# First projection of a hybrid transformer layer in two halves of its contraction, with tokens loaded first

## The reference, cut to what matters

```python
mod = silu(c) @ w_ada + b_ada
shift1, scale1, gate1, shift2, scale2, gate2 = split(mod, 6)
h = rmsnorm(x, norm1_g) * (1.0 + scale1) + shift1
proj = h @ w_in                       # q, v, forget gates, output gate, u (conv), branch gates
```

## Time and profile before

| | us |
|---|---|
| median of 3 runs | 834.47 |
| range of them | 833.5 to 837.01 |
| profiled execution, its own time | 835.81 |
| its span, first to last instruction | 834.0 |

### The profile page before, as it was taken

One profiled execution on the slowest core, in us unless ns is written; L12 is line 12 of the kernel. 1 busy time (PEld: TensorE's weight loads), 2 busy tenths in 40 slices (PEclk: granted clock), 3 DMA queues, 4 the chain that ended last, 5 costly groups with the idle time before them and its releaser, 6 DMA issues.

```text
span 834.0 us, 12875 instructions
## 1 busy us (share of the span) xinstructions
PE 793.0 (95%) x5234; PEld 545.1 (65%) x5234; DVE 381.6 (46%) x773; ACT 236.2 (28%) x400; POOL 20.9 (3%) x22
## 2 busy tenths in 40 slices
PE   4999999999999999999999999799999999989984
PEld 2779897999999999965555455354554745445222
DVE  1176999879987755583232312212222112112114
ACT  3163747344445353231111111111111101011001
POOL 1000010100000100100000000000000000000000
PEclk9999999999999999999999999999999999999998
DMA  8998797523442479869999999999999999999995
GB/s 331 408 362 332 283 410 293 194 101 103 152 152 101 152 236 372 369 233 423 391 425 426 421 426 426 422 425 426 421 427 420 422 423 425 423 425 425 426 420 202
DMA packets 81221, 284.71 MB, mean 341 GB/s; under 512 B 5256, under 2 KB 12040, under 8 KB 64520
## 3 DMA queue, kind: packets, MB, share of 16 engines
q1 hardware_dynamic: 80664, 282.55, 85.2%
q10 hardware_dynamic: 496, 1.30, 0.4%
HBM read 280.67 MB, written 3.16 MB: 340 GB/s over the span
## 4 chain that ended last, share of the span: by engine, by line
PE 64%; SPq 18%; DMA 11%; DVE 2%; issue 2%; ACT 1%; POOL 0%; DVEq 0%; POOLq 0%
SPq L628 14%; PE bank L2112 13%; PE bank L2168 7%; PE bank L1727 6%; PE bank L1729 6%; PE bank L1732 6%; DMA chunk<-in_w_expert_down 5%; PE bank L2019 3%; PE bank L1996 3%; PE bank L1789 3%; PE bank L1713 3%; PE bank L1771 3%; DMA chunk<-in_w_expert_gate_up 2%; PE bank L1674 2%; DMA ring<-in_w_out 2%
## 5 line engine op out<-in xcount | busy, mean ns | idle before, releaser
L2112 PE MATMUL bank<-chunk,xg 128*64 128x512 f32 (+2 forms) x1024 | 196.9, 602 | 8.9 <-DMA chunk<-in_w_expert_gate_up 8.7
L2112 PEld LDWEIGHTS bank<-chunk,xg 128*64 128x64 f32 (+2 forms) x1024 | 62.2, 127 | 136.9 <-issue 121.9
L2168 PE MATMUL bank<-chunk,act_t 128*64 128x512 f32 (+2 forms) x480 | 98.2, 620 | 3.7 <-DMA chunk<-in_w_expert_down 3.6
L1526 DVE SCALAR_TENSOR_TENSOR act_r<-bank,w_slot,sil 128x256 f32<-128x256 f32 x26 | 12.6, 484 | 166.1 <-ACT sil L995 166.1
L1538 DVE TENSOR_TENSOR y_lo<-bank,y_hi 128x512 fp32r<-128x512 f32 x52 | 35.8, 691 | 76.5 <-ACT y_hi L1008 76.5
L995 ACT ACTIVATE sil<-bank 128x256 f32<-128x256 f32 x26 | 10.0, 384 | 194.7 <-PE bank L2112 194.7
L1090 DVE TENSOR_TENSOR ring_lo<-ring,ring_hi 128x1024 fp32r<-128x1024 f32 x44 | 52.9, 1219 | 23.5 <-ACT ring_hi L777 23.3
L2168 PEld LDWEIGHTS bank<-chunk,act_t 128*64 128x64 f32 (+2 forms) x480 | 30.0, 131 | 51.2 <-issue 50.3
L1008 ACT ACTIVATE y_hi<-bank 128x512 fp32r<-128x512 f32 x52 | 30.9, 597 | 104.8 <-PE bank L2168 100.4
L1150 DVE SCALAR_TENSOR_TENSOR conv<-upad,dw,conv 128x256 f32<-128x256 f32 x120 | 52.8, 512 | 0.0
L777 ACT ACTIVATE ring_hi<-ring 128x1024 fp32r<-128x1024 f32 x44 | 44.4, 1054 | 27.3 <-PE bank L1753 12.6
(11 more groups left out here) (316 smaller groups left out, 1205.6 us busy)
## 6 DMA issues: line engine op xcount, KB each, us to landing
chunk<-in_w_expert_gate_up SPq DMA_DIRECT2D x128, 1024.0 KB, 20.2
chunk<-in_w_expert_down SPq DMA_DIRECT2D x63, 1024.0 KB, 22.3
ring<-in_w_in SPq DMA_DIRECT2D x16, 2048.0 KB, 9.7
ring<-in_w_ada SPq DMA_DIRECT2D x12, 2048.0 KB, 9.8
ring<-in_w_proj_hgrn SPq DMA_DIRECT2D x2, 2048.0 KB, 7.6
ring<-in_w_out SPq DMA_DIRECT2D x2, 2048.0 KB, 14.1
ring<-in_w_proj_conv SPq DMA_DIRECT2D x1, 2048.0 KB, 7.7
chunk<-in_w_shared_gate_up SPq DMA_DIRECT2D x2, 1024.0 KB, 22.8
```

Of the source, the lines that this page charges most:

```text
L2112: ins = mm(bank[2 + b][row:row + width, :], xg[:, k, c:c + width], w[:, k % 4, :], start=(k == 0), stop=(k == KD - 1))
L2168: ins = mm(out[row:row + width, :], act_t[:, c, row:row + width], w[:, c, h * 512:(h + 1) * 512], start=(c == 0), stop=(c == 1))
```

## The change

The contraction of `u1` is done in two halves. The first (k 0 to 3) needs only the scale of ada2, the second (k 4 to 7) that of ada3. So ada2 and ada3 get groups, partial banks, copies, sums and modulations of their own. The tokens are loaded ahead of ada2, and u1 ahead of ada3. On ScalarE the sigmoid goes behind the squares; on VectorE the scaling of the sum goes ahead of the silu; on TensorE the partial of ada2 goes behind h0 and h1. The counts of semaphores move with it. The diff, cut to its core:

```diff
-        ADA_GROUPS = ((0, 2), (2, 2), (4, 8))
+        ADA_GROUPS = ((0, 1), (1, 1), (2, 2), (4, 8))
...
-        for name in ("ada2", "ada3", "u1", "ada0", "ada1", "u2", ...
+        for name in ("ada2", "u1", "ada3", "ada0", "ada1", "u2", ...
+        place["u1"], place["ada3"] = 2, 1
@@ SP
-            load_block("ada2")
             for s, x in enumerate((A["x_prompt"], A["x_sample"])):
                 sp.dma_start(x_tok[:, s, :], x[0]).then_inc(s_x, 16)
+            load_block("ada2")
@@ ScalarE
-            act.wait_ge(vec_copied, 1)
-            nc.scalar.activation(csig, vec[:, R_C:R_C + 16], ACT.Sigmoid).then_inc(c_sig, 1)
...
             act.wait_ge(s_x, 32)
             for s in range(NS):
                 own.mark(nc.scalar.activation(xn[:, s, :], x_tok[:, s, :], ACT.Square, accum_out=ssq[:, s:s + 1]))
+            act.wait_ge(vec_copied, 1)
+            nc.scalar.activation(csig, vec[:, R_C:R_C + 16], ACT.Sigmoid).then_inc(c_sig, 1)
...
             copy_partials(0)
             act.wait_ge(s_init, 3)
-            act.wait_ge(gain1_done, 2)
             for j in (1, 3):
+                act.wait_ge(gain1_done, j + 1)
                 filled(act, f"h{j}")
...
                 ins.then_inc(act_evac, 1)
+                if j == 1:
+                    copy_partials(1)
...
             evacuate_u1(0)
-            copy_partials(1)
-            act.wait_ge(mod_done, 4)
+            copy_partials(2)
+            act.wait_ge(mod_done, 6)
@@ VectorE
+            dve.wait_ge(own_act, 2)
+            V.tensor_scalar(ssq, ssq, 1.0 / D, EPS, ALU.mult, ALU.add).then_inc(ssq_ready, 1)
             dve.wait_ge(vec_copied, 2)
             dve.wait_ge(c_sig, 1)
...
-            dve.wait_ge(own_act, 2)
-            V.tensor_scalar(ssq, ssq, 1.0 / D, EPS, ALU.mult, ALU.add).then_inc(ssq_ready, 1)
             dve.wait_ge(rms_ready, 1)
...
-            modulation(8, 16, 1, 2)
-            (gain1 of k 0 to 7, both kinds of token)
             for j in (0, 2):
+                modulation(8 + 2 * j, 12 + 2 * j, 1 + j // 2, 2 + j)
+                (gain1 of k 2j to 2j + 3, both kinds of token)
+                dve.wait_ge(gain1_done, 2 + j)
                 filled(dve, f"h{j}")
@@ TensorE
-            pe.wait_ge(vec_copied, 2)
-            pe.wait_ge(c_silu, 1)
-            ada_partial(0)
             pe.wait_ge(s_x, 32)
             for j in range(4):
                 to_channels((f"xt{j}", 0), x_tok, j).then_inc(proj_ready, 1)
             pe.wait_ge(xn_done, 2)
-            ada_partial(1)
             for j in range(2):
                 to_channels((f"h{j}", 0), xn, j).then_inc(proj_ready, 1)
-            ada_sums(0)
+            pe.wait_ge(vec_copied, 2)
+            pe.wait_ge(c_silu, 1)
+            ada_partial(0)
             for j in range(2, 4):
                 to_channels((f"h{j}", 0), xn, j).then_inc(proj_ready, 1)
+            ada_sums(0)
...
-            project("u1", x_gained, before_k=lambda k: evacuated(pe, f"h{k // 2}"), after_k=ada_within_u1)
-            pe.wait_ge(mod_done, 5)
+            arrived("u1")
+            u1_quarter(0, range(0, 4))
+            u1_quarter(1, range(0, 4))
+            u1_quarter(2, range(0, 4))
+            ada_partial(1)
+            u1_quarter(3, range(0, 2))
+            ada_sums(1)
+            u1_quarter(3, range(2, 4))
+            u1_quarter(0, range(4, 8))
+            ada_partial(2)
+            u1_quarter(1, range(4, 8))
+            u1_quarter(2, range(4, 8))
+            ada_partial(3)
+            u1_quarter(3, range(4, 6))
+            ada_sums(2)
+            u1_quarter(3, range(6, 8))
+            pe.wait_ge(mod_done, 7)
```

More of the change, by code:

```diff
@@ L342, in build @@
         blocks = []
-        for name in ("ada2", "ada3", "u1", "ada0", "ada1", "u2", "ada4", "q0", "ada5", "zf0", "ada6", "zb0", "ada7", "q1", "ada8", "zf1", "ada9", "zb1",
+        for name in ("ada2", "u1", "ada3", "ada0", "ada1", "u2", "ada4", "q0", "ada5", "zf0", "ada6", "zb0", "ada7", "q1", "ada8", "zf1", "ada9", "zb1",
                      "ada10", "v0", "ada11", "v1", "og0", "og1", "ga0", "ga1", "gb0", "gb1"):
@@ L802, in _ @@
             split_hi(1, (0, 1))
-            act.wait_ge(mod_ready, 2)
+            act.wait_ge(mod_ready, 3)
             for j in range(2):
@@ L846, in _ @@
             act.wait_ge(u_gated, 2)
-            copy_partials(2)
+            copy_partials(3)
             split_hi(split.index("v1"), range(4))
@@ L868, in _ @@
                     if n < 2:
-                        act.wait_ge(mod_ready, 3)
+                        act.wait_ge(mod_ready, 4)
                     else:
@@ L1090, in split_lo @@
                     V.tensor_tensor(part_lo(n, q), tile_of(split[n])[:, :, q * P:(q + 1) * P], part_hi(n, q).bitcast(F32), ALU.subtract).then_inc(w_lo_done, 1)
-            modulation(8, 16, 1, 2)
[L1093 to L1096, removed]
-            for j in (0, 2):
+            for j in (0, 2):
+                modulation(8 + 2 * j, 12 + 2 * j, 1 + j // 2, 2 + j)
+                for s in range(NS):
+                    V.scalar_tensor_tensor(gain1.rearrange("p (k s) -> p k s", s=NS)[:, 2 * j:2 * j + 4, s], mod_v[:, M_SC1 + 2 * j:M_SC1 + 2 * j + 4, s], 1.0,
+                                           vec[:, R_G1 + 2 * j:R_G1 + 2 * j + 4], ALU.add, ALU.mult).then_inc(gain1_done, 1)
+                dve.wait_ge(gain1_done, 2 + j)
                 filled(dve, f"h{j}")
@@ L1104, in _ @@
                 ins.then_inc(dve_evac, 1)
-            modulation(0, 8, 2, 4)
+            modulation(0, 8, 3, 6)
             dve.wait_ge(s_pad, 2)
@@ L1199, in og_gate @@
                     ins.then_inc(dve_evac, 1)
-            modulation(16, 48, 3, 7)
+            modulation(16, 48, 4, 9)
             gains(gain2, M_SC2, R_G2)
@@ L1667, in ada_partial @@
                 arrived(f"ada{ADA[j]}")
-                if g == 2 and j == first:
-                    pe.wait_ge(part_copied, 1)
+                if g >= 2 and j == first:
+                    pe.wait_ge(part_copied, g - 1)
                 w = tile_of(f"ada{ADA[j]}")
@@ L1790, in scores, with u1_quarter @@
                     ins.then_inc(sc_ready, 1)
[L1792 to L1799, removed]
-            project("u1", x_gained, before_k=lambda k: evacuated(pe, f"h{k // 2}"), after_k=ada_within_u1)
-            pe.wait_ge(mod_done, 5)
+            def u1_quarter(q, ks):
+                b = open_fill("u1", q // 2) if (q % 2, ks[0]) == (0, 0) else fill_bank("u1", q // 2)
+                w = tile_of("u1")
+                for k in ks:
+                    if q == 0:
+                        evacuated(pe, f"h{k // 2}")
+                    ins = mm(b[:, (q % 2) * T:(q % 2 + 1) * T], w[:, k, q * P:(q + 1) * P], x_gained[:, k, :],
+                             start=(q % 2 == 0 and k == 0), stop=(q % 2 == 1 and k == KD - 1))
+                if q % 2 and ks[-1] == KD - 1:
+                    ins.then_inc(proj_ready, 1)
+            arrived("u1")
[15 more added lines that the diff above has]
+            pe.wait_ge(mod_done, 7)
             for k in range(KD):
@@ L1822, in _ @@
                 if level == -1:
-                    ada_sums(2)
+                    ada_sums(3)
                 quarter(name, 1)
@@ L1850, in _ @@
                 if level == 3:
-                    pe.wait_ge(mod_done, 7)
+                    pe.wait_ge(mod_done, 9)
                     nc.tensor.transpose(bank[7][0:NS * KD, 0:P], mod_v[:, M_SH2:M_SH2 + KD, :].rearrange("p k s -> p (k s)"), ident)
```

## The result

| | before | changed |
|---|---|---|
| median of 13 runs, us | 834.87 | 839.54 |
| range, us | 833.5 to 838.58 | 836.38 to 845.45 |
| profiled execution: its time / span, us | 835.81 / 834.0 | 838.06 / 836.2 |

The account below looks back on a forecast made before the run. TensorE bounds the kernel to 300 us, DMA from 380; the end of the shift's sums sets u2. Those sums end at 44.5 instead of 41.3, 3.2 us later: span 837.2, median 837.7 us, range 833.5 to 841.0.

Parts of the forecast that it names:

- The chain: From token landing through xn, u1 and the shift's sums to u2: u2 at 49.6 us, 3.2 us later.
- the clock rose in the middle of the partial: Ahead of u1: TensorE's durations shorten midway through ada2's partial, taken as 2.8 us; u1 begins at 22.8 us.
- The DMA queues: Loads behind the reordered blocks: later waits on SP's queue were costed at nothing, covered by a backlog of loads.
- The table load: On ScalarE between squares and sigmoid: a second load of 1.28 us in the chain, taken as 1.3, xn at 14.3.
- slower: Outcome class: more than 0.5% (4.2 us) slower than before; chance 0.27.
- rival B: The 2.3 us idle ahead of u2 drops TensorE's clock: +2.0 us, 839.7; chance 0.22 together with the slow case.
- 1.85 from the end of the sums to the first matmul: Ahead of u1: time from the end of ada2's sums to u1's first matmul, a 1.85 us term.
- 1.37 us idle at 44.99 was followed by no drop: Argument against rival B: in the kernel before, TensorE's idle ahead of u2 left the clock at 1.00 from 46.5 us.
- A: Ahead of u1: no second table load, or TensorE fast early; u1 at 19.9 to 21.5, time 834.8 to 836.4; chance 0.28.
- C: u1 begins on its weights at 18.4 us, so 833.3 us, faster; chance 0.06.
- D: At the first loads: the tokens are kept back by 2 us or more, so 840 us; chance 0.04.

Follow-up runs that it names:

- r1: The changed kernel again, word for word, with a second profile; median 838.83 us, ratio 1.0069 to the kernel before.
- r9: The kernel before with only the partial of ada1 and the shift's sums earlier inside u1, no load moved, no split; median 834.29 us, ratio 0.9982.
- r7: r6 with r2's early sigmoid and the partials and sums inside u1 moved earlier; median 833.85 us, ratio 0.9987.
- r10: The changed kernel with r7's order inside u1 and nothing else; median 838.64 us, ratio 1.0038.
- r2: The changed kernel with one sigmoid of a constant column ahead of the squares, so its table is loaded first; 839.13 us, ratio 1.0038.
- r3: The changed kernel with filler matmuls on TensorE, 11 at the start and 7 between the token transposes and xn; 838.02 us, ratio 1.0040.
- r4: The changed kernel with nine filler matmuls of 256 columns in TensorE's wait ahead of u2; 839.11 us, ratio 1.0058.
- r8: r7 with two filler matmuls ahead of u1 and three ahead of u2; 833.97 us, ratio 0.9982.
- r12: r11 with five filler matmuls in the lengthened wait ahead of u2; median 836.12 us, ratio 1.0006.
- r6: The changed kernel with the partial of ada2 ahead of h0 and h1, and the sums ahead of h2 and h3; median 837.62 us, ratio 1.0029.
- r11: The kernel before with an extra ScalarE copy of 1024 columns, lengthening TensorE's wait ahead of u2, left open; median 837.20 us, ratio 1.0035.
- r5: The changed kernel with filler matmuls in three waits: four ahead of u1, one at half of the contraction, five ahead of u2; 838.83 us, ratio 1.0043.

## Why the prediction was right, and where it fell short

**The chain was right, step by step.** The tokens came at 8.1 as said, the table load of 1.28 us stood between square and sigmoid, xn ended at 14.1 (14.3 forecast), h0 and h1 took 1.97 (1.84), the partial 2.3 (2.8), `u1` started at 22.1 (22.8). That the clock rose in the middle of the partial, as was assumed, is in part luck: in r1 it had risen before h0, and `u1` started at 21.3. From there to the end of the sums it took 22.1 us, 4.9 more than before (4.5 forecast, the rest being gaps between the shorter pieces). The sums ended at 44.2 (44.5) and `u2` started at 49.2 (49.6), 5.06 us behind them. That this end and not that of `u1` sets the time is shown by r9, r7 and r10: the sums moved, `u2` followed until TensorE's own queue held it. The DMA queues cost nothing, as said; TensorE has no wait for a load behind `u1`.

**The table load.** The row of 1.28 us with the next activation 0.01 us behind it agrees with the earlier trace rows; r2 took the load away and gained 1.3 us ahead of `u1`. The square at the front brought a table without the sigmoid. The Trainium skill (ScalarE: Activation LUTs, What ACT_TABLE_LOAD costs) puts a switch at about 2.66 us; the trace does not agree, with 1.29 us from the start of the load to the next activation.

**What fell short is the sum**: a shift of 3.2 us and a median of 837.7 were forecast, 4.7 us and 839.54 measured (the median of the kernel before moved from 834.47 to 834.87 with more executions). That is inside the range, but over the 0.5% bound, to which "slower" had 0.27. The chain gave 2.9 of it, a little less than forecast; the missing 1.8 us go with the clock, rival B's mechanism. Four things in it were off. It was priced as an alternative with a chance of 0.22, when it is a tail that belongs in the median. It was looked for ahead of `u2` alone. The sum itself had two more waits in it that were new or longer, without calling them a danger: the "1.85 from the end of the sums to the first matmul", all of it idle now, while before h2 and h3 stood in it, and the wait from the token transposes to xn, 2.4 us in the trace. r2, r3, r4 and r10 show falls ahead of `u1`, r4 and r10 behind the wait for xn. And "1.37 us idle at 44.99 was followed by no drop" was read as evidence against it. Waits of 1.85 to 2.4 us are another matter than one of 1.37: r8 shows that filling waits up to 1.4 us gains nothing to speak of, r12 that filling one of 2.3 does. Last, it took a fall behind `u2`'s wait to cost 2.0 us; by the work further on, the two that were seen cost 1.3 (r2) and 1.1 (r3).

An estimate from the profiles comes near the missing amount. Of the six in which the wait ahead of `u1` is 1.85 us and open (the changed kernel's first, r1, r2, r3, r4, r10), four have a fall there, of 1.5, 3.0, 1.6 and 1.7 us: 1.3 us on the mean. Of the six in which the wait ahead of `u2` is 2.2 to 2.3 us and open (the changed kernel's first, r1, r2, r3, r6, r11), two have one: 0.4 us. Together 1.7; but six profiles are few.

**The other rivals.** A: the second load was there; the early rise of the clock did come in r1, where `u1` started at 21.3, within its 21.2 to 21.5. C and D did not come: `u1` started 3.8 us after its weights could be there, and the tokens landed first.

**Where the gain of the split went.** `u1` does start two us sooner. But the partial and the sums of `ada3`, done before in idle time, now stand inside it (1.85 and 0.8 us), the sums of the shift have 0.9 us more of `u1` ahead of them, and 0.8 us of a new wait come in; the rest of the 4.9 us, about 0.5, are gaps between the shorter pieces. r6 shows that 2.2 to 3 us ahead of `u1` can be had back by TensorE's order alone, r7 that the order inside gives 1.6 more. r9 has the same result as r7 without moving a load or splitting anything: no time shows a gain of the split itself (further on, in the profiles, r7 is 0.3 us ahead of r9).

**Left open:** how much of the tail comes from each of the three waits. r5, with the last two filled, is 0.9 us below the changed kernel in the mean, on another chip and with overlapping intervals. r6, with 2.24 us ahead of `u2` and 1.8 and 0.8 us elsewhere, lies 1.9 us above the kernel before in the mean though its `u2` is not later, so the wait ahead of `u2` has most likely a part; r10, with only that one shortened, keeps the width of 9 us, so the others have one. The wait ahead of xn was filled in no run that kept a comparable rest (r3's seven fillers did not reach: TensorE stays idle for 2.5 us there). Nor was it tried which wait between 1.4 and 1.85 us is the longest harmless one.

## What to carry to other kernels

Splitting a contraction so that it can start earlier pays only if the step that the next stage waits for comes earlier; look for the last end that the chain names (here four small matmuls and what follows them) and move that first. Before an edit is priced, list the new waits of TensorE and how long each is: in this kernel one wait of 2.3 us cost 2.0 us more on the mean when it was left open than when it was filled (interval 0.3 to 3.8), and a median of few runs or one profile hides that. Work that is ready (r6's h2 and h3), or even a filler (r12), belongs in such a wait.

## What the runs showed of the hardware

- TensorE's granted clock went to 0.50 (1.2 GHz) around the end of waits of 1.85 to 2.4 us, from 0.6 us before work was taken up again (r3, near 20 us) to 1.7 us after it (r2, near 50.6 us), in some executions and not in others; the low stretches of the first 56 us were 3 to 7 us long. The Trainium skill (TensorE: Matmul & The Clock Gate, Part 1) says that the number of matmuls at the low clock at the start of one kernel differs from execution to execution. Two profiles of the changed kernel agree: h0, h1 and the partial took 1.97 + 2.32 us in one and 1.09 + 1.85 in the other (r1).
- At the start of the span the granted clock reads 1.00 while matmuls take twice their time: the token transposes took 3.67 us in the changed kernel, 1.97 in r3 behind fillers.
- A table load took 1.28 us of ScalarE, and the activation behind it began 0.01 us later, in the changed kernel as at the Silu.
